# Hybrid decoder step on one core: eight more projection slabs inside the cache window, the last batch written out, and a sixth slot in the ring of loads

## What is computed

```python
h = h + 0.5 * swiglu(rms_norm(h, g_ffn1), w_ffn1_gate, w_ffn1_up, w_ffn1_down)   # 5632 wide
u = rms_norm(h, g_mix) @ w_in                    # q | k | v | conv input, 40 tiles of 128 columns
q, k, v, c_in = split(u)                         # 8 heads, two maps of 64 for q and k, 128 for v
# differential attention with ALiBi; prompt: causal over 256
w = softmax(s)[..., 0, :] - lam * softmax(s)[..., 1, :]
# sample: keys and values of 16 pages of 128 for each of 8 batches, found by page_table, and 8 new
o_attn = rms_norm(w @ v, g_subln) * (1 - lam_init)
# conformer: GLU, causal depthwise conv of 31 taps, group norm over 8 groups of 128 channels, swish
y = silu(group_layer_norm(conv31(a * sigmoid(g)) + b_dw))
h = h + concat(o_attn, y) @ w_out
h = h + 0.5 * swiglu(rms_norm(h, g_ffn2), ...)
h = h + (p @ w_ple_proj) * sigmoid(rms_norm(h, g_ple) @ w_ple_gate)
y_out = rms_norm(h, g_final)                     # k, v and the conv state are outputs too
```

## Time and profile before

| | us |
|---|---|
| median of 3 runs | 2714.27 |
| the runs | 2712.66 to 2714.98 |
| the profiled execution: own time | 2711.31 |
| its span | 2709.5 |
| PE busy | 2611.9 (96% of the span) |
| DVE, ACT, POOL busy | 1497.4, 942.0, 354.3 |

### The profile page before, as it was taken

One profiled execution on the slowest core, in us unless ns is written; L12 is line 12 of the kernel. 1 busy time (PEld: TensorE's weight loads), 2 busy tenths in 40 slices (PEclk: granted clock), 3 DMA queues, 4 the chain that ended last, 5 costly groups with the idle time before them and its releaser, 6 DMA issues.

```text
span 2709.5 us, 49989 instructions
## 1 busy us (share of the span) xinstructions
PE 2611.9 (96%) x20082; PEld 2542.3 (94%) x20082; DVE 1497.4 (55%) x2082; ACT 942.0 (35%) x1075; POOL 354.3 (13%) x630
## 2 busy tenths in 40 slices
PE   7999999999999999988887899999999999999997
PEld 7999999999999999977775899999999999999997
DVE  5555555555555644467786345555555555555655
ACT  5222322223222332354555433222222222222433
POOL 2000000000000120066865010000000000000323
PEclk9999999999999999999999999999999999999998
DMA  5444444444444455799999844444444444444342
GB/s 231 156 143 152 155 141 153 146 149 154 145 149 152 142 185 200 284 377 365 377 375 382 305 155 144 152 150 145 155 147 147 154 142 153 151 143 155 140 145 81
DMA packets 92112, 506.37 MB, mean 187 GB/s; under 512 B 10401, under 2 KB 10402, under 8 KB 51298
## 3 DMA queue, kind: packets, MB, share of 16 engines
q1 hardware_dynamic: 90866, 496.59, 50.5%
q0 software_dynamic: 1136, 8.32, 0.9%
HBM read 495.63 MB, written 9.23 MB: 186 GB/s over the span
## 4 chain that ended last, share of the span: by engine, by line
PE 89%; DMA 3%; ACT 2%; SPq 2%; issue 2%; POOL 1%; DVE 1%; POOLq 0%; DVEq 0%; ACTq 0%
PE bank L1589 26%; PE bank L1590 26%; PE bank L1591 26%; PE bank L1675 2%; PE bank L1677 2%; PE bank L1676 2%; DMA raw<-k_pool 2%; PE bank L1715 1%; PE bank L1764 1%; SPq L427 1%; POOL ssq L518 1%; SPq L422 1%; PE bank L1741 1%; ACT x_hi L666 1%; DMA raw<-v_pool 1%
## 5 line engine op out<-in xcount | busy, mean ns | idle before, releaser
L1589 PE MATMUL bank<-x_hi,w_hi 128*128 128x320 f32 x3584 | 1111.6, 310 | 17.0 <-DVE w_lo L1046 10.9
L1590 PE MATMUL bank<-x_lo,w_hi 128*128 128x320 f32 x3584 | 1109.9, 310 | 0.0
L1591 PE MATMUL bank<-x_hi,w_lo 128*128 128x320 f32 x3584 | 1109.7, 310 | 0.0
L1037 DVE TENSOR_TENSOR w_lo<-raw,w_hi 128x2048 fp32r<-128x2048 f32 x309 | 707.7, 2290 | 305.8 <-ACT w_hi L648 291.0
L648 ACT CAST w_hi<-raw 128x2048 fp32r<-128x2048 f32 x294 | 559.6, 1903 | 838.2 <-PE bank L1591 838.2
L1589 PEld LDWEIGHTS bank<-x_hi,w_hi 128*128 128x128 f32 x3584 | 674.9, 188 | 19.0 <-issue 13.6
L1590 PEld LDWEIGHTS bank<-x_lo,w_hi 128*128 128x128 f32 x3584 | 675.1, 188 | 0.2
L1591 PEld LDWEIGHTS bank<-x_hi,w_lo 128*128 128x128 f32 x3584 | 674.9, 188 | 0.0
L1589 PE MATMUL bank<-mid_hi,w_hi 128*128 128x320 f32 x1408 | 435.3, 309 | 1.0 <-DVE w_lo L1037 1.0
L1591 PE MATMUL bank<-mid_hi,w_lo 128*128 128x320 f32 x1408 | 435.1, 309 | 0.0
L1590 PE MATMUL bank<-mid_lo,w_hi 128*128 128x320 f32 x1408 | 435.1, 309 | 0.0
(11 more groups left out here) (215 smaller groups left out, 2011.7 us busy)
## 6 DMA issues: line engine op xcount, KB each, us to landing
raw<-slabs_ffn SPq DMA_DIRECT2D x264, 1024.0 KB, 4.7
raw<-k_pool SPq DMA_DIRECT2D x128, 512.0 KB, 6.5
raw<-v_pool SPq DMA_DIRECT2D x128, 512.0 KB, 6.4
raw<-slabs_in SPq DMA_DIRECT2D x48, 512.0 KB, 7.8
raw<-slabs_ple SPq DMA_DIRECT2D x18, 1024.0 KB, 4.8
raw<-slabs_in SPq DMA_DIRECT2D x16, 1024.0 KB, 4.8
raw<-slabs_out SPq DMA_DIRECT2D x16, 1024.0 KB, 4.8
h<-x_t SPq DMA_DIRECT2D x4, 640.0 KB, 8.1
```

What stands on the lines that cost most here:

```text
L1037: vt.tensor_tensor(w_lo[n % 2][:, :, :], raw[n % 4][:, :].rearrange("p (k n) -> p k n", n=P), w_hi[n % 2][:, :, :].bitcast(F32), ALU.subtr ...
L1589: mm(out, w_hi[w2][:, t, :], xh, start=start, stop=False)
L1590: mm(out, w_hi[w2][:, t, :], xl, start=False, stop=False)
L1591: return mm(out, w_lo[w2][:, t, :], xh, start=False, stop=stop)
```

## The change

`N_PRE` is 8: the dense stage holds the q slabs only. The window has 32 slabs. Pass 0 has the 8 k slabs, read by DVE into kT (`read_k`), pass 1 the 8 v slabs beside the scores of batch 1 and the values of batch 0, and passes 2 to 7 the 16 convolution slabs in the same periods of three groups. The two passes write to D_BANK and G_BANK in turn; all v tiles are transposed in H_BANK. `queries(3)` comes ahead of channel 0's taps on POOL.

The ring has five slots up to the first keys of batch 2 (`SIXTH`), which go to a sixth one. It lies where the third pair of split buffers was: halves 0 to 31 use three pairs, later ones two (`split_buffer`). From then on a unit takes the slot of the unit six before (`ring_slots`).

Batch 7's values, the former pass 8, are written out. There are two buffers for its transposed exponentials (`ET_b`, in the place of kT's end), so that turns run ahead of `weigh`. Channel 7's taps from 8 on, its norm and swish stand there too; of its 31 sample taps POOL does 23 and DVE the other 8 (`sample_rest`). PE starts output slab 0 right behind the last values, with `combine(7)`, channel 7's mean and variance and the sample's sum between its matmuls and channel 7's tile (k = 15) last. The splits of the input are cut otherwise: channels 0-3, 4-6, 7 and heads 0-6, 7. The load "O" comes two units earlier.

```diff
-N_PRE = 16
+N_PRE = 8
 N_WIN = N_IN - N_PRE
-RING = 5
-WBUF = 3
+RING = 6
+HALVES_3 = 32
...
+POOL_TAPS = 23
...
-    if it == 0:
-        return (2 * q, 2 * q + 1)
-    c, r = divmod(4 * (it - 1) + q, PERIOD)
-    return (8 + 2 * c + r,) if c < 8 and r < 2 else ()
+    if it < 2:
+        return (8 * it + 2 * q, 8 * it + 2 * q + 1)
+    c, r = divmod(4 * (it - 2) + q, PERIOD)
+    return (16 + 2 * c + r,) if c < 8 and r < 2 else ()
...
+SIXTH = RING_AT["K", 2 * KV_SLOTS]
...
+    return n % 3 if n < HALVES_3 else n % 2
...
+        slot = n % (RING - 1) if n < SIXTH else RING - 1 if n == SIXTH else slot_of[n - RING]
...
+        ET_b = place("ET_b", [P, 2, 4, P], offset=qk_at + 4 * HEADS * NTOK)
...
-            pool.wait_ge(evacuated, E(S_IN + 15))
+            pool.wait_ge(d_read, HEADS)
             pool.dma_start(k_t, kT[:, :, :]).then_inc(stored, 16)
...
-                if n < WBUF:
+                if n < 3:
                     act.wait_ge(slab_done, S_OUT - 1 if n < 2 else S_OUT)
                 else:
-                    act.wait_ge(half_mm, n - WBUF + 1)
+                    act.wait_ge(half_mm, n - (3 if n < HALVES_3 else 2) + 1)
...
                     if r == 0 and 0 <= c - 1 < 8:
                         head_root(c - 1)
-                    if r == 0 and c < 8:
-                        half_up(2 * (9 + 2 * c))
+                    if r == 1 and c < 8:
+                        half_up(2 * (17 + 2 * c) + 1)
                     if r == 2 and c + 1 < 8:
-                        slab_up(8 + 2 * (c + 1))
+                        slab_up(16 + 2 * (c + 1))
...
+            slab_upper(0)
+            copy_ET(b, 3)
+            sigmoid_tables()
+            conv_sigmoid(6)
+            exp_tables()
+            out_read(b)
+            heads_upper(7, 8, "heads_b")
+            conv_upper(4, 7, "conv_b")
+            sample_root(0, G_BANK)
             sample_square(1)
+            sample_upper(0, "sample_a")
             sample_root(1, H_BANK)
             sample_upper(1, "sample_b")
+            conv_square(7)
             slab_upper(1)
+            conv_root(7)
+            sigmoid_tables()
+            conv_sigmoid(7)
+            exp_tables()
+            conv_upper(7, 8, "conv_c")
...
+            def read_k(j):
+                dve.wait_ge(half_mm, 2 * j + 2)
+                vt.tensor_tensor(kT[:, j, :], (G_BANK if j % 2 else D_BANK)[:, 0:NTOK], rinv[:, :], ALU.mult
+                                 ).then_inc(d_read, 1)
...
+            for q in range(GROUPS):
+                if q == 0:
+                    slab_low(9)
+                read_scores(1, q)
+                if q:
+                    slab_low(9 + 2 * q)
+                read_v(2 * q)
+                slab_low(10 + 2 * q)
+                read_v(2 * q + 1)
...
+            slab_lower(0)
+            for k in range(POOL_TAPS, TAPS):
+                taps(7, k, k + 1)
+                if k == 28:
+                    conv_swish(6)
+                sample_rest(k)
+            heads_lower(7, 8, "heads_b")
+            out_store(b)
+            conv_lower(4, 7, "conv_b")
+            sample_scale(0)
+            conv_center(7)
+            sample_lower(0, "sample_a")
             sample_scale(1)
             sample_lower(1, "sample_b")
+            conv_scale(7)
             slab_lower(1)
+            conv_swish(7)
+            conv_lower(7, 8, "conv_c")
...
+            for q in range(GROUPS):
+                score(1, q)
+                if q:
+                    turn(0, q)
+                slab_half(8 + 2 * q, 0)
...
+                slab_whole(9 + 2 * q)
+                v_turn(2 * q)
+                if q < GROUPS - 1:
+                    weigh(0, q)
...
+            score_new(1)
+            v_turn(7)
+            weigh(0, 3, (0,))
+            weigh_new(0)
+            weigh(0, 3, (1,))
...
+                    order = [k for k in OUT_ORDER if k != KD - 1] + [KD - 1]
+                for n, k in enumerate(order):
+                    if j == 0:
+                        if n == 2:
+                            combine(NB - 1)
+                        if k in FIRST_USE:
+                            pe.wait_ge(xo_lo, XO[FIRST_USE[k]])
+                        if n == 5:
+                            conv_mean(7)
+                        if n == 6:
+                            sample_sum(1, H_BANK)
+                        if n == 9:
+                            conv_var(7)
```

More of the change, by code:

```diff
@@ L119, with split_buffer, ring_slots @@
 RING_AT = {what: n for n, what in enumerate(ORDER)}
-OUT_SLOT = (0, 3, 1, 2)
-assert RING_AT["O", 0] % RING == OUT_SLOT[0]
+SIXTH = RING_AT["K", 2 * KV_SLOTS]
+def split_buffer(n):
+    return n % 3 if n < HALVES_3 else n % 2
+def ring_slots():
+    slot_of, held, taken, last = [], [], [], {}
+    for n in range(len(ORDER)):
+        slot = n % (RING - 1) if n < SIXTH else RING - 1 if n == SIXTH else slot_of[n - RING]
+        slot_of.append(slot)
+        held.append(last.get(slot))
+        taken.append(slot_of.count(slot))
+        last[slot] = n
+    return slot_of, held, taken
+SLOT_OF, HELD, TAKEN = ring_slots()
+OUT_SLOT = (1, 2, 3, 0)
+assert SLOT_OF[RING_AT["O", 0]] == OUT_SLOT[0]
 TURN_AT = {0: 0, 1: 2, "new": 4, 2: 6, 3: 8}
@@ L212, in hymba_step @@
         S_p = place("S_p", [P, 2, 3 * P], offset=h_at + 2 * KCOLS * 4)
-        ring = raw + [place("raw4", [P, SLAB * P], offset=w_at + 3 * 4 * SLAB * P)]
+        ring = raw + [place(f"raw{4 + i}", [P, SLAB * P], offset=w_at + o * 4 * SLAB * P) for i, o in enumerate((3, 1))]
         wh_at = [w_at + 4 * SLAB * P * i for i in (0, 2, 1)]
@@ L445, in _ @@
             for n, (kind, at) in enumerate(ORDER):
-                slot = n % RING
+                slot = SLOT_OF[n]
                 if kind == "S":
@@ L728, in _ @@
                     root(1)
-            with act.Fori(1, 3) as i:
-                for j in range(4):
-                    split_next(S_IN, i, j)
             for j in range(3):
-                split_next(S_IN, 3, j)
+                split_next(S_IN, 1, j)
             def exp_tables():
@@ L1161, in _ @@
                 for j in range(4):
-                    split_next(S_IN, i, j)
+                    if not (i == 1 and j == 3):
+                        split_next(S_IN, i, j)
                     if i == 0 and j == 2:
@@ L1411, in _ @@
             dve.wait_ge(consts, 2)
-            for it in range(1, NB + 1):
+            for it in range(2, NB):
                 b = it - 1
@@ L1650, in _ @@
                     sum_features(1)
-            with pe.Fori(1, 4) as i:
-                for j in range(4):
-                    pe.wait_ge(evacuated, E(S_IN + 4 * i + j - 4))
-                    dense(S_IN + 4 * i + j, j, j)
+            for j in range(4):
+                pe.wait_ge(evacuated, E(S_IN + j))
+                dense(S_IN + 4 + j, j, j)
             pe.wait_ge(consts, 2)
@@ L1886, in _ @@
                         head_sum(c)
-            combine(NB - 1)
-            sample_sum(1, H_BANK)
+            b = NB - 1
+            combine(b - 1)
+            turn(b, 0)
+            turn(b, 1)
+            weigh(b, 0)
+            turn(b, "new")
+            turn(b, 2)
+            weigh(b, 1)
+            weigh_new(b)
+            turn(b, 3)
+            sample_sum(0, G_BANK)
+            weigh(b, 2)
+            weigh(b, 3)
             for j in range(4):
```

304 lines of the change are left out of this document (165 added, 139 removed).

## The result

The changed kernel takes 2728.40 us (median of five runs, 2727.31 to 2731.56), the kernel before took 2714.24 us in the same session (2712.66 to 2714.98). The ratio is 1.0057, interval 1.0046 to 1.0068: the change makes the kernel slower by 0.57%, 14 us. Forecast were 2686 us, between 2672 and 2703. The profiled execution has a span of 2725.5 us.

What follows compares the result with a forecast made beforehand. PE was taken to bound the dense stages and DMA mostly the window. Terms: -18.9 at T, -15 sixth slot, +6 last batch, sum -27.9, from 2711.3 to 2683.4 us; with 3.0 for the median 2686, range 2672 to 2703.

Steps and rivals of the forecast that it cites:

- The moved slabs: Stage before the window: 8 k slabs leave it, so the window starts at 1010.4 in place of 1066.0, -55.6 us.
- Pass 0: Window's first pass: keeps 8 slabs, its v turns go to pass 1; 66.2 us in place of 68.6, -2.4.
- Pass 1: New mixture of keys, 8 v slabs and values, bound by PE: +82.7 us, with a 3 us stall before v turn 7.
- Rival (c): Pass 1 is bound by the ring, PE waiting for each group's second slab: slower, 2733 us; chance 0.05.
- The sixth slot and the two buffers: Passes 2 to 7: values' slots free some 8 us earlier, -15 us (0 to -25); two split buffers cost nothing in steady state.
- so 310.8 us stay: Passes 2 to 7 hold the 16 convolution slabs as 1 to 6 did, same time before the slot's gain; old pass 7's 43.6 go.
- Rival (a): The sixth slot gives nothing in passes 2 to 7, as DMA is at its limit already: 2701 us; chance 0.20.
- side remark on DMA: Pass 2 to T: the skill's 358 GB/s per core would give 347 us and 2715 in all; rejected by 411 GB/s measured.
- The last batch: Pass 8 and output slab 0: 1 us shows up to T, then 17 us against 12.65 costs 5; +6 us (0 to +12).
- T: Time point of batch 7's last value matmul, at 1511.6 us in the earlier trace; forecast near 1478.
- the sign of its fall: Forecast falls if passes 2 to 7 still take 311 us, PE waits for slabs in pass 1, or slab 0 ends over 22 us after T.
- chances for a faster kernel: Below 2708.9 us: the forecast (0.63), (a), (d) at 2670 us (0.05), half of (b), channel 7's end backing up (0.07); said as 0.87.

Runs made afterwards that it cites:

- experiment 2: Changed kernel with the old five slots and three split buffers, but the gate slab's splits left late as in the changed kernel: 2736.73 us, ratio 1.0082.
- experiment 4: Changed kernel with only slot assignment altered: two loads behind a gate slab take the slots of the values behind it, the third the gate slab's: 2706.00 us, ratio 0.9973.
- experiment 1: Changed kernel with its ring part undone: five slots, three split buffers, both gate slab halves split in the earlier group: 2708.24 us, ratio 0.9981.
- experiment 6: Kernel of experiment 5 with the gate slab's second half also split some microseconds sooner, at the end of the group ahead: 2695.33 us, ratio 0.9919.
- e8: Kernel of experiment 6 with one product in three of the slabs in passes 2 to 7 left out (256 matmuls), all bytes kept; measuring only: 2675.24 us, one run.
- experiment 5: Kernel of experiment 4 with only head 7's square root on ACT moved to the head of the last batch: 2699.72 us, ratio 0.9940.
- experiments 1 to 7: The seven follow-up kernels that do all the work, varying ring, split times, slot order and last batch of the changed kernel: 2694.27 to 2736.73 us.

## Why the prediction was wrong, point by point

**The moved slabs** (forecast -55.6 at the window's start): measured 1066.0 - 1012.6 = -53.4. Of the missing 2.2 us, 0.5 lie ahead of query tile 7's copies (DVE read the tile at 1009.64, where the earlier trace rows have 1009.15). The rest is in the copies, which I took over from the earlier trace rows at 0.24 us:

```profile
1010.27 1.08 POOL L575 COPY Qb<-qT 64x64 f32<-64x64 f32 x1 [43.05 <-DVE qT L1215]
1011.42 1.12 POOL L577 COPY Qb<-qT 64x64 f32<-64x64 f32 x1
1012.60 0.23 POOL L575 COPY Qb<-qT 64x64 f32<-64x64 f32 x1
```

```profile
1010.05 2.39 DVE L1255 TENSOR_TENSOR wh_lo<-raw,wh_hi 128x1024 fp32r<-128x1024 f32 x2
```

The step took their duration from a place where DVE did nothing beside them. Here they lie on the path and beside DVE's first split, and take four times as long; the next copy, behind the split, takes 0.23 again. That the split is the reason follows from this coincidence alone; no run moved it away.

**Pass 0** (forecast 66.2): 68.9. The first scores come after PE has stood for 2.7 us and run at half the clock (granted 0.50 from 1012.6 to 1016.0, 1.2 GHz), and that group takes 18.9 us; the others take 16.14, as computed.

**Pass 1** (forecast 82.7 with a stall of 3 us before the last v turn): 81.9, PE busy 79.56 at 315 GB/s, where 319 were worked out. The stall is there, in its place and with its releaser:

```profile
1160.12 0.55 PE L1792 MATMUL bank<-ident,tmp 128*128 128x128 f32 x3 [2.16 <-DVE tmp L1315]
```

A stretch that no trace had shown was costed to 1% out of its parts. Rival (c) is refuted.

**The sixth slot and the two buffers** (forecast -15 and 0): here the prediction failed. The step was "With six slots they take the slot of a slab or of keys, which is free some 8 us earlier", and right behind it "The two split buffers cost nothing in steady state: a group's second half of a slab is converted one group after the first, and the wait (the half two before) is over when the old group ends." The second sentence has the cause in it and asks the wrong waiter. With two buffers the gate slab's second half can only be split after the half two before has been multiplied, and the change moved that split into the next group. I asked whether PE would wait for the half; it doesn't. The half lies in a ring slot until it is split, and SP waits for the slot. In the kernel before both halves were split a group sooner, which is where my "8 us earlier" came from; I read a release time from before for a step that the change moves. The price is in experiment 2, 31.1 us with five slots, and in experiment 4, 22.2 us with six. The claim that the gain "can't be below nothing by this mechanism" was wrong by the same omission, and so no rival ended there: the only slower one was (c), with a chance of 0.05.

The slots were told too simply as well. Before, in passes 2 to 6, values take a slot of values in two groups of three; in the third the first unit takes the gate slab's slot (V14 that of slab 13). With six slots only the first unit of a group takes the slot of keys or of a slab. The second takes that of values (V13 that of V10) or, once in three groups, the gate slab's (V17 that of slab 19), and that is the load that stood.

A second step was off by less: "so 310.8 us stay". With the old ring put back the six passes took 316.5 us (experiment 1), 5.7 more, and why is open.

What the slot is worth by itself is less sure. The 15 us were three fifths of 25, with the reason that DMA is named in both of SP's waits; the earlier trace rows name PE and DVE, so the share was a guess. With the late split the slot is worth 12.4 us (experiment 2 against the changed kernel). With no load standing behind the late split the passes take 313.0 us in experiment 4 and 304.4 in experiment 6, against 316.5 in experiment 1, 3.5 and 12.1 us less, and the last figure also has the sooner split in it. No run has five slots with the sooner split and the new order of release, so how much of this is the slot's isn't shown. Rival (a), that it gives nothing, isn't ruled out by such a run; its reason, that DMA is at its limit, is, by the 386 GB/s of experiment 6 against the 370 of before.

Its side remark on DMA can be sharpened. The kernel of e8 moves 404 GB/s for 290.5 us with a share of 1.02, that of 6 moves 386 for 304.4 us. The Trainium skill, "DMA: Bandwidth & Descriptors", section "Where 436 GB/s comes from", has about 358 GB/s for each core as what binds between HBM and SBUF; both measurements stand above it over some 300 us, and below the 425 GB/s that the prediction took from the page for a core that streams alone.

**The last batch** (forecast +1 up to T, 17 us behind T): 20.2 us up to T, less than the 22.6 of before, and 20.65 from T to DVE's first read of the output at 1539.45. (17 less the 12.65 of before is 4.35, of which the prediction made 5.) Of the two, the first was priced too high by 3.4 us and the second too low by 3.7. The row that I had not foreseen is the wait of 6.75 us shown in experiment 5, an order on ACT that made DVE's list late; moving one root gave 5.7 us back (experiment 5). What I had named, the split of output slab 1 ahead of the swish, is there as well:

```profile
1534.48 2.28 DVE L1466 TENSOR_TENSOR w_lo<-raw,w_hi 128x2048 fp32r<-128x2048 f32 x1
1536.69 0.48 DVE L1378 SCALAR_TENSOR_TENSOR u_p<-tmp,vec,sig 128x256 f32<-128x256 f32 x1
...
1539.45 0.49 DVE L1612 SCALAR_TENSOR_TENSOR h<-bank,h 128x320 f32<-128x320 f32 x1 [0.86 <-issue]
```

**The sum.** T was forecast at 1010.4 + 66.2 + 82.7 + 295.8 + 23.6 = 1478.7 and came at 1518.8: 2.2 + 2.7 - 0.8 + 39.4 - 3.4 = 40.1 us late. Of the 39.4, experiment 4 shows 22.2 to be the blocked load, and the sooner split together with it (304.4 us, experiment 6) brings 30.8; the remaining 8.6 us lie between a slot's gain that may not have come in full and the 5.7 us of experiment 1, and stay open. What the prediction named as the sign of its fall, passes 2 to 7 at 311 us or more, was the right thing to look at. Its chances for a faster kernel add up to 0.63 + 0.20 + 0.05 and half of 0.07, which is 0.915 and not 0.89 at most.

## What to carry to other kernels

When a change delays a step, list everyone who waits for what the step sets free (the buffer that it writes, the buffer that it reads, and the queue behind whoever waits for either), and not only for its result. In a ring that is handed out in the order of its loads, one slot released late stops every load behind it, with five slots as with six: put the late slot's turn behind those that come free before it, or bring its release forward, before paying for another slot. And a release time read from the old trace holds only for steps that the change leaves where they are.

## What the runs showed of the hardware

Small copies on POOL of 64 x 64 elements took 1.08 and 1.12 us while DVE ran two splits of 1024 elements in each partition (2.39 us for both), and 0.23 us directly behind them; the first two took the same 1.08 and 1.12 us in the kernels of experiments 1 to 7. The other thing is the rate that the loads reach when no slot is late: 386 GB/s over 304 us with all the work (experiment 6), and 404 GB/s over 290 us, with DMA's share at 1.02, where PE had one product in three less (e8). The kernel before had 370 over its 310.8 us, and 411 only over 22.6 us.
